# Two-block transformer kernel: the turned left operands of 256-column matmuls lie 64 bytes lower in each partition, with their eight chunks in the opposite order

## The reference

```
def _swiglu(x, wg, wu, wd):
    return (jax.nn.silu(x @ wg) * (x @ wu)) @ wd        # 1024 -> 2816 -> 1024

def _recurrent_mixer(h, w_in, ...):
    u = h @ w_in                                        # 1024 -> 2048
    ...
for layer in range(DEPTH):
    h = h + 0.5 * _swiglu(_rmsnorm(h, norm_ffn1[layer]), ...)
    h = h + mixer(_rmsnorm(h, norm_mix[layer]))
    h = h + 0.5 * _swiglu(_rmsnorm(h, norm_ffn2[layer]), ...)
```

## Time and profile before

| | us |
|---|---|
| median of 3 runs | 1684.77 (1684.06 to 1688.99) |
| the profiled execution | 1683.63 |
| its span, first to last instruction | 1681.8 |
| PE busy | 1450.6 |
| DVE busy | 861.2 |
| ACT busy | 623.1 |
| mean granted TensorE clock | 0.952 of full speed |

### The profile page before, as it was taken

How to read it: one execution, slowest core, us unless ns; L and a number is a source line. 1 busy time by engine, 2 the same in 40 slices (tenths; PEclk the granted TensorE clock), 3 DMA queues, 4 the chain that set the end, 5 groups by cost and what they waited for, 6 DMA issues and landing times.

```text
span 1681.8 us, 27002 instructions
## 1 busy us (share of the span) xinstructions
PE 1450.6 (86%) x10956; PEld 1195.1 (71%) x10956; DVE 861.2 (51%) x1583; ACT 623.1 (37%) x1062; POOL 36.5 (2%) x48
## 2 busy tenths in 40 slices
PE   7987765688967665799999689999999998889998
PEld 6865432356744332699987469999899998789997
DVE  5664110167641101655558865555655558765555
ACT  5471110154611100544431454344444437654343
POOL 0000000001000000100000000000000000000000
PEclk9998988798989988999999889999999999999999
DMA  9728999993299999954554225544545552545510
GB/s 390 325 89 347 388 426 428 429 427 163 101 391 400 428 427 428 386 191 168 191 202 151 100 100 201 196 167 187 186 170 196 200 200 101 200 170 194 197 53 26
DMA packets 31618, 408.74 MB, mean 243 GB/s; under 512 B 3456, under 2 KB 5632, under 8 KB 7216
## 3 DMA queue, kind: packets, MB, share of 16 engines
q1 hardware_dynamic: 29088, 404.34, 60.6%
q10 hardware_dynamic: 2448, 3.24, 0.6%
HBM read 406.50 MB, written 1.06 MB: 242 GB/s over the span
## 4 chain that ended last, share of the span: by engine, by line
PE 72%; DMA 15%; DVE 8%; ACT 3%; issue 1%; POOL 0%; POOLq 0%; SPq 0%; DVEq 0%; ACTq 0%
DMA ring<-stream 15%; PE bank L1795 10%; PE bank L1799 10%; PE bank L1796 10%; PE bank L1826 9%; PE bank L655 5%; PE bank L1832 4%; PE bank L1574 3%; PE bank L1592 3%; PE bank L661 2%; PE bank L596 2%; PE bank L1931 2%; PE bank L623 1%; PE bank L1505 1%; PE bank L2151 1%
## 5 line engine op out<-in xcount | busy, mean ns | idle before, releaser
L514 DVE TENSOR_TENSOR unit_lo<-ring,unit_hi 128x1024 fp32r<-128x1024 f32 x324 | 394.8, 1225 | 332.1 <-ACT unit_hi L509 331.8
L509 ACT ACTIVATE unit_hi<-ring 128x1024 fp32r<-128x1024 f32 x324 | 341.5, 1061 | 458.9 <-PE bank L1799 294.9
L1795 PE MATMUL bank<-hT_hi,unit_hi 128*128 128x256 f32 x1408 | 347.3, 284 | 4.7 <-DVE norm_lo L446 4.4
L1796 PE MATMUL bank<-norm_lo,unit_hi 128*128 128x256 f32 x1408 | 346.3, 283 | 0.0
L1795 PEld LDWEIGHTS bank<-hT_hi,unit_hi 128*128 128x128 f32 x1408 | 270.1, 192 | 10.8 <-issue 5.5
L1796 PEld LDWEIGHTS bank<-norm_lo,unit_hi 128*128 128x128 f32 x1408 | 270.5, 192 | 3.1
L1799 PE MATMUL bank<-hT_hi,unit_lo 128*128 128x256 f32 x1408 | 197.6, 283 | 0.0
L1799 PEld LDWEIGHTS bank<-hT_hi,unit_lo 128*128 128x128 f32 x1408 | 181.6, 192 | 0.0
L1574 PE MATMUL bank<-ring,work 128*32 128x256 f32 x1792 | 121.2, 423 | 52.1 <-DMA ring<-stream 52.1
L1574 PEld LDWEIGHTS bank<-ring,work 128*32 128x32 f32 x1792 | 59.2, 119 | 109.6 <-DMA ring<-stream 68.2
L1826 PE MATMUL bank<-unit_hi,act_lo 128*128 128x512 f32 x336 | 131.9, 393 | 0.0
(11 more groups left out here) (310 smaller groups left out, 1897.9 us busy)
## 6 DMA issues: line engine op xcount, KB each, us to landing
ring<-stream SPq DMA_DIRECT2D x180, 2048.0 KB, 12.2
work<-ahead SPq DMA_DIRECT2D x4, 2048.0 KB, 9.9
ahead<-ahead SPq DMA_DIRECT2D x4, 2048.0 KB, 17.7
kept_slot<-ahead SPq DMA_DIRECT2D x2, 2048.0 KB, 25.2
ring<-stream SPq DMA_DIRECT2D x4, 512.0 KB, 7.7
work<-spread ACTq DMA_DIRECT2D x2, 1024.0 KB, 12.1
x<-x_in SPq DMA_DIRECT2D x2, 512.0 KB, 4.7
work<-final_rows ACTq DMA_DIRECT2D x2, 512.0 KB, 7.7
```

The lines of the kernel that those rows point to most:

```text
L509: nc.scalar.activation(high_buf(name, u), raw_unit(name, u), ACT.Copy).then_inc(hi_done, 1)
L514: low = nc.vector.tensor_tensor(low_buf(name, u), raw_unit(name, u), high_buf(name, u).bitcast(F32), ALU.subtract)
L1795: nc.tensor.matmul(out, high[:, k, :], hT_hi[:, k, :], start=(k == 0), stop=False)
L1796: nc.tensor.matmul(out, high[:, k, :], norm_lo[:, k, :], start=False, stop=False)
```

## The change

`near_hi` and `near_lo` are the same size as `hT_hi` and `norm_lo` and start 64 bytes lower, at 114816 and 123008. Chunk k lies in place 7-k of them, so the chunk that is written last is the lowest and the one that reaches into the last 64 bytes of `xn`, whose columns have been turned by then. They are used for the inputs of the four feed-forward stages and of `r_in` (norms n4, n6, n7, n8, n9): `split_evac` writes them, and the 256-column matmuls read them. The 512-column matmuls of the other stages go on with `hT_hi`, `norm_lo` and `cat_lo`. The third pair of `rec_units` moves up by 160 bytes, to 201920 and 206016; both leave 192 when divided by 256. No instruction is added, removed or reordered on any engine, and every shape stays.

```diff
+NEAR = 64
...
+        near_hi = nc.alloc_sbuf_tensor_at("near_hi", [P, KD, T], F32R, offset=hT_base - NEAR)
+        near_lo = nc.alloc_sbuf_tensor_at("near_lo", [P, KD, T], F32R, offset=cat_base - NEAR)
...
-                     for b, (base, at) in enumerate(((kept_base, 0), (kept_base, 2 * UNIT), (work_base, 12312)))]
+                     for b, (base, at) in enumerate(((kept_base, 0), (kept_base, 2 * UNIT), (work_base, 12352)))]
...
+        NEAR_TURNS = ("n4", "n6", "n7", "n8", "n9")
+
+        def near(left, k):
+            return left[:, KD - 1 - k, :]
...
-                src, high = bank[g % 4][:, kk * T:(kk + 1) * T], hT_hi[:, k, :]
+                src = bank[g % 4][:, kk * T:(kk + 1) * T]
+                if name in NEAR_TURNS:
+                    high, low = near(near_hi, k), near(near_lo, k)
+                else:
+                    high, low = hT_hi[:, k, :], left_lo[:, k, :]
...
-                    nc.tensor.matmul(out, high[:, k, :], hT_hi[:, k, :], start=(k == 0), stop=False)
-                    nc.tensor.matmul(out, high[:, k, :], norm_lo[:, k, :], start=False, stop=False)
+                    nc.tensor.matmul(out, high[:, k, :], near(near_hi, k), start=(k == 0), stop=False)
+                    nc.tensor.matmul(out, high[:, k, :], near(near_lo, k), start=False, stop=False)
                 low_ready(pe, name, u, it)
                 for k in range(KD):
-                    mm = nc.tensor.matmul(out, low[:, k, :], hT_hi[:, k, :], start=False, stop=(k == KD - 1))
+                    mm = nc.tensor.matmul(out, low[:, k, :], near(near_hi, k), start=False, stop=(k == KD - 1))
```

More of the change, by code:

```diff
@@ L435, in split_evac @@
                 eng.wait_ge(turn_hi, TURN_DONE[g][1])
-            low = cat_lo if name.startswith("cat") else norm_lo
+            left_lo = cat_lo if name.startswith("cat") else norm_lo
             for kk in range(2):
                 k = 2 * j + kk
-                src, high = bank[g % 4][:, kk * T:(kk + 1) * T], hT_hi[:, k, :]
+                src = bank[g % 4][:, kk * T:(kk + 1) * T]
[3 more added lines that the diff above has]
+                    high, low = hT_hi[:, k, :], left_lo[:, k, :]
                 gain = None if name.startswith("cat") else gains[:, int(name[1:]), k:k + 1]
@@ L443, in split_evac @@
                 elif gain is None:
-                    last = nc.vector.tensor_tensor(low[:, k, :], src, high.bitcast(F32), ALU.subtract)
+                    last = nc.vector.tensor_tensor(low, src, high.bitcast(F32), ALU.subtract)
                 else:
-                    last = nc.vector.scalar_tensor_tensor(low[:, k, :], src, gain, high.bitcast(F32), ALU.mult,
+                    last = nc.vector.scalar_tensor_tensor(low, src, gain, high.bitcast(F32), ALU.mult,
                                                           ALU.subtract)
```

## The result

The changed kernel takes 1671.37 us (median of 4 runs, 1670.15 to 1673.03) against 1685.98 us for the kernel before (median of 4 runs): ratio 0.9918, 95% interval 0.9899 to 0.9937. It is 14.6 us faster by the medians, where 30 were forecast; the time lies inside the range of 1632 to 1690, outside the forecast mechanism's own of 1645 to 1665. The profiled execution took 1672.35 us, its span 1670.6.

The account below looks back on a forecast made before the run. PE's distance between matmul starts was taken to bound the kernel. Gains of 27.7 + 1.6 + 0.5 + 0.3 = 30.1 us took the profiled 1683.63 to 1653.5, or 1655 us on the median's scale; range 1632 to 1690.

Parts of the forecast that it names:

- the forecast mechanism: 256-column matmuls: the step falls by half or so, to 111 to 115.5 ns; time 1655 us, chance 0.30.
- What bounds the kernel: Feed-forward stages: PE is busy for all 170.00 us of twenty tiles; it stays alone at the bound, so all gain arrives.
- That the operands' position changes the step, with the third buffer pair as witness: Last mixer's input projection: a misaligned third-pair unit steps at 117.1 ns, an aligned one takes 2.88 us against 2.81.
- That the chunk order costs nothing: Evacuations into the new tensors: descending chunk order shifts addresses by multiples of 1024 bytes, claimed indifferent, 0 us.
- The output projection's 0.1 us a unit: Last mixer's output projection: third-pair units come into line, 2.82 to 2.72 us each, some 0.3 us gained for three.
- The input projection's 1.6 and 0.5 us: Last mixer: ten aligned units gain 1.6 us; five third-pair units go from 117.1 to 113.3 ns, gaining 0.5 us.
- the term of 27.7 us: Feed-forward stages: 4128 matmuls of 256 columns step at 113.3 ns instead of 120, gaining 27.7 us.
- The midpoint of the floor and 117.1: Feed-forward 256-column step: 113.2 ns, midway between the 109.2 ns one-pass floor and the measured misaligned step, supporting 113.3.
- C: 256-column matmuls: a small gain as with the third pair, 117.1 ns a step, 13.0 us gained, 1672 us; chance 0.15.
- D: 256-column matmuls: only the place within 64 bytes matters, so the step stays 0.120 us and nothing is gained, 1685 us; chance 0.25.
- E: 256-column matmuls: operand reads meet more often at 64 bytes, each step 8 ns slower, 1720 us; chance 0.17.
- B: 256-column matmuls: the step reaches the one-pass floor of 109.2 ns, gaining 48.4 us, 1636 us; chance 0.13.

Follow-up runs that it names:

- experiment 1: Changed kernel with distance 0, keeping chunks from last to first and the third buffer pair in line; ratio 0.9992 to the kernel before.
- experiment 2: Changed kernel with the turned input 64 bytes higher instead of lower, chunks in rising order; ratio 0.9959 to the kernel before.
- experiment 3: Changed kernel with the turned input 128 bytes higher instead of 64 lower, chunks in rising order; ratio 1.001 to the kernel before.
- experiment 5: Changed kernel with the turned input lower by 192, 320, 96, 32 bytes in ffn0 to ffn3; steady tiles 8.413, 8.373, 8.440, 8.447 us.
- experiment 6: Changed kernel with the turned input lower by 128, 160, 224, 256 bytes in ffn0 to ffn3; steady tiles 8.520, 8.527, 8.347, 8.500 us.
- experiment 7: Changed kernel with act_hi and act_lo higher by 32, 128, 192, 96 bytes in ffn0 to ffn3; tiles 8.247, 8.225 and 8.429 alternating, 8.213, 8.447 us.

## Why the prediction was right and wrong

*What bounds the kernel:* right. PE stayed alone at the bound in the feed-forward stages, and all that its step lost arrived in the tile. In the mixer's first half there is now one wait on the low part of a unit, which I had not forecast: I had read ACT's and DVE's slack in the feed-forward stages only. In the second profile of the changed kernel, where the second half steps at 113.3 ns too, that half also waits (unit 13 takes 2.96 us, unit 14 2.85). (Of the two lines in the earlier trace rows only ACT's names PE; DVE's idle time ended with ACT's high part.)

*That the operands' position changes the step, with the third buffer pair as witness:* right, and shown for the input's position at fixed weights (experiments 1 to 3, 5, 6). That only the position of the two against each other counts is not shown: no run moved both together. *That the chunk order costs nothing:* right (experiment 1). *The output projection's 0.1 us a unit:* right for the units whose rows were read (unit 4 2.72 us against 2.82, unit 5 2.72 against 2.76); over the whole projection 0.1 us arrived rather than 0.3 (three units at 0.1 and 0.04 would have been 0.4). *The input projection's 1.6 and 0.5 us:* 0.8 arrived, since its second half ran in the slow rhythm and one unit of the first half waited.

*The size of the step, the term of 27.7 us:* this is the step that failed. I wrote "I take 113.3", and 113.3 ns does exist at 64 bytes, but in the feed-forward stages only until the first 512-column matmuls; the steady step is 117.8. The term measured 4 stages x 20 tiles x 48 x 2.2 ns = 8.4 us, and the 512-column matmuls, to which I had given no term, gave 80 x 0.027 = 2.2 more; 0.5 goes off, since the first step of a tile is no longer the short one. That makes the 10.1 us of the twenty tiles; the second tiles, three of the four at 113.3 ns, add 1.1. The error behind it: I treated the step as a function of the addresses of the two operands. It is one of a rhythm too, which passes from one matmul to the next. The trace of before had a sign of it in the place I took my number from: the step behind the 512-column matmuls was 0.11 us and the next ones 0.12, at equal distances. I read it as a step that the pair of lines can keep up, where it was only the first one behind 512-column matmuls. The midpoint of the floor and 117.1 was no evidence either; that 113.3 ns turned up to the digit is partly luck.

*The rivals:* C, 1672 us, had the right time and nearly the right step (117.1), as a copy of the third pair. The time is partly luck: its 12.0 us for the feed-forward steps were 8.4 in the steady tiles, and what the 512-column matmuls gained is not in its sum. D (only the place within 64 bytes counts) falls with the change itself. E's 8 ns a step appear nowhere; 128 and 160 bytes do make the tiles longer than before, but only at 8.520 and 8.527 us. B's floor of 109.2 ns appears in no run.

*The Trainium skill's rule of two independent read ports* ("TensorE: Matmul & The Clock Gate", Part 2, step 1) would have made the positions indifferent, and they are not: with the input moved by 64 bytes and nothing else, the same matmuls take 117.8 or 113.3 ns instead of 120.0. Which resource is behind it no run here shows.

**What stays open:** why the positions matter. The runs give a period of 256 bytes, the steps, and that a rhythm is carried on; they do not show which resource is behind it, nor why 96 bytes on one side is not the 96 bytes on the other, nor whether moving both operands together would change nothing. What picks the rhythm where a stretch starts is open too: two profiles of one kernel differ in it. A stretch without any 512-column matmuls is in the record, the input projection: once picked, a rhythm holds there, 113.3 ns in its first half and 117.8 in its second.

## What to carry to other kernels

When dense float32r matmuls at full clock start further apart than the columns they stream, compare the operands' start bytes modulo 256: a shift of one pair of tensors by 64 bytes adds no instruction and was worth 0.7 to 0.8%, and 1.5% with a second pair placed too. Not every shift helps: 128 and 160 bytes made the tiles longer. Try several distances in one kernel, one for each repeated stage, and read the tile length of each from one profile. Do not take the step of an address pair from the first matmuls of a stretch, and measure neighbours together: the placement of one group's operands changes the pace of the next group.

## What the runs showed of the hardware that was not expected

- Two steady rhythms at the same distance, 113.3 and 117.8 ns for float32r matmuls of 256 columns at full clock and a distance of 64 bytes; each holds for dozens of matmuls.
- With the weights in place, the pace goes by the input's distance modulo 256 bytes: 64 and 320 lower give tiles of 8.373 us, 192 lower and 64 higher 8.413, 0 and 256 give 8.500.
- An operand's position changes the speed of matmuls that never read it (experiment 7: the 256-column step is 113.3 ns with `act_hi` and `act_lo` 192 bytes higher, 117.8 with 96).
- At half clock the 256-column step is 213 ns with a distance of 64 bytes and without.
- No float32r step of 256 columns settled below 113.3 ns in any run, 6.6 ns over the 106.7 that is half of the half clock's 213.3, while plain float32 has a surplus of 2.5.
